# A routed-expert encoder trunk on one core: modulation sums in column quarters, and a router written with comparisons and one scan

## The reference

```python
mod = cond @ w_ada[layer] + b_ada[layer]            # 6 x 1024 values a layer
sh1, sc1, g1, sh2, sc2, g2 = jnp.split(mod, 6, axis=-1)
h = modulate(rms_norm(x, norm1_g[layer]), sh1, sc1)
x = x + g1 * mixer(h)                               # layer 0 attention, layer 1 convolution module
h = modulate(rms_norm(x, norm2_g[layer]), sh2, sc2)
x = x + g2 * moe_ffn(h, ...)
```

## Time and profile before

| | us |
|---|---|
| median of the 3 runs (2121.23 to 2124.85) | 2123.42 |
| the profiled execution, its own time | 2121.78 |
| its span from first to last instruction | 2119.7 |
| PE busy in the span | 1919.2 (91%) |
| DVE busy | 1201.3 (57%) |
| ACT busy | 493.6 (23%) |
| POOL busy | 303.2 (14%) |

### The profile page before, as it was taken

The page is one execution under the profiler, slowest core; times in us unless marked ns, Lnnn a source line. Parts: engine busy times, 40 slices in busy tenths (PEclk is TensorE's granted clock), DMA queues, the critical chain, the costliest instruction groups (busy, mean ns, idle before and its releaser), DMA issues.

```text
span 2119.7 us, 49706 instructions
## 1 busy us (share of the span) xinstructions
PE 1919.2 (91%) x19544; PEld 1163.5 (55%) x19544; DVE 1201.3 (57%) x2175; ACT 493.6 (23%) x1042; POOL 303.2 (14%) x464
## 2 busy tenths in 40 slices
PE   5999999999999946999999579999899399999990
PEld 3444444455666634777777457655445266666660
DVE  3466600378899764333433469999994534333436
ACT  3101100356777630000000230000544000000002
POOL 0001030000000012222222400000001122222223
PEclk9999999799999977999999789999999699999995
DMA  9466520100440087877985803033107599864446
GB/s 397 164 248 256 211 61 0 41 11 11 160 159 11 11 332 264 298 263 260 351 329 216 311 30 105 1 117 107 50 0 267 203 407 407 325 239 170 169 171 253
DMA packets 122490, 391.41 MB, mean 185 GB/s; under 512 B 23808, under 2 KB 44928, under 8 KB 118272
## 3 DMA queue, kind: packets, MB, share of 16 engines
q1 hardware_dynamic: 72432, 303.48, 37.9%
q0 software_dynamic: 21904, 66.99, 8.7%
q10 hardware_dynamic: 28032, 19.17, 3.0%
HBM read 337.33 MB, written 47.49 MB: 182 GB/s over the span
## 4 chain that ended last, share of the span: by engine, by line
PE 84%; DVE 8%; DMA 4%; ACT 1%; issue 1%; SPq 0%; POOL 0%; ACTq 0%; DVEq 0%; POOLq 0%
PE ps L1578 23%; PE ps L1588 12%; PE ps L1420 10%; PE ps L1633 10%; PE ps L1473 5%; PE ps L1529 5%; PE ps L1487 4%; PE ps L1500 4%; PE ps L1512 4%; DVE kv L1302 3%; PE ps L1705 3%; DMA kv<-in_w_ada 1%; PE ps L1670 1%; PE ps L1399 1%; ACT hT L639 1%
## 5 line engine op out<-in xcount | busy, mean ns | idle before, releaser
L1578 PE MATMUL ps<-kv,hT 128*32 128x256 f32 x5504 | 387.2, 380 | 3.4 <-DMA kv<-in_w_gate_up 3.4
L1302 DVE SCALAR_TENSOR_TENSOR kv<-kv,cols 128x640 f32<-128x640 f32 (+1 forms) x330 | 266.2, 807 | 11.2
L1578 PEld LDWEIGHTS ps<-kv,hT 128*32 128x32 f32 x5504 | 229.8, 111 | 77.0 <-issue 5.2
L1176 DVE TENSOR_TENSOR hT<-hT,modc 128x256 f32<-128x256 f32 x146 | 62.1, 425 | 303.8 <-PE ps L1578 303.7
L1633 PE MATMUL ps<-hT,ring 128*128 128x320 f32 (+1 forms) x768 | 225.4, 455 | 6.3 <-ACT hT L639 6.3
L1420 PE MATMUL ps<-hT,ring 128*128 128x512 f32 x512 | 224.5, 597 | 1.6 <-ACT hT L639 1.6
L745 ACT ACTIVATE hT<-ps 128x128 f32<-128x128 f32 x146 | 40.4, 277 | 759.2 <-PE ps L1578 759.2
L1012 DVE TENSOR_TENSOR_SCAN pbuf<-hT 128x128 f32<-128x128 f32 (+7 forms) x128 | 173.2, 1353 | 47.0 <-ACT hT L690 46.7
L1633 PEld LDWEIGHTS ps<-hT,ring 128*128 128x128 f32 x768 | 146.3, 192 | 81.9 <-ACT hT L639 6.9
L1578 PE MATMUL ps<-ring,hT 128*32 128x256 f32 x2560 | 150.6, 387 | 19.7 <-issue 18.0
L1420 PEld LDWEIGHTS ps<-hT,ring 128*128 128x128 f32 x512 | 98.0, 192 | 124.2 <-issue 121.2
(11 more groups left out here) (260 smaller groups left out, 2439.4 us busy)
## 6 DMA issues: line engine op xcount, KB each, us to landing
kv<-in_w_gate_up SPq DMA_DIRECT2D x136, 512.0 KB
kv<-in_w_ada SPq DMA_DIRECT2D x21, 2048.0 KB, 8.1
ring<-in_w_gate_up SPq DMA_DIRECT2D x80, 512.0 KB
kv<-in_w_down SPq DMA_DIRECT2D x48, 512.0 KB
ring<-in_w_down SPq DMA_DIRECT2D x40, 512.0 KB
hT<-in_w_gate_up SPq DMA_DIRECT2D x40, 512.0 KB
expert_rows<-hT ACTq DMA_DIRECT2D x584, 32.0 KB
ring<-in_w_in SPq DMA_DIRECT2D x32, 512.0 KB, 11.3
```

What stands on the lines that cost most here:

```text
L1302: ins = V.scalar_tensor_tensor(new, old, w_dw_c[:, c, k:k + 1], new, ALU.mult, ALU.add)
L1578: ins = mm(bank(0)[UNIT * q:UNIT * (q + 1), 0:2 * P], xT[:, c, :], wset[s][q // 2][:, 512 * c + 256 * (q % 2):512 * c + 256 * (q % 2) + 25 ...
```

## The change

In the modulation, DVE sums four pieces into four buffers (`ada_sum[k]`), and PE takes four at a time: four matmuls with 32-wide weights `ones[:, 0:32]`, each into 32 of the 128 PSUM partitions, after chunks 4, 7, 9, 12 and 14 of Q and K. ACT copies the whole bank, POOL stores four rows. In the router, an expert's rank in its group is the count of the three others that beat it (six comparisons, one reduction), both picked experts come from it at once, the running sum is one scan, and both choices' rows are worked in one instruction. The 0/1 matrices are made 32 wide on the `low` side; PE multiplies them in 128 matmuls with 32-wide weights, a quarter of the table each. PE reads eight of its 16 registers ahead of the table matmuls and eight behind. The matrices move to `hT` below the third weight set; the other scratch stays in `spare`. `square(1, t)` writes to `ring` instead of `bcB` for t below 7, so POOL's reload of `bcB` waits for `x_made`, and SP's load of expert 0's down weights waits for `sq_done`.

```diff
+ADA_GROUPS = REST_ADA // 4
+GROUP_AFTER = (4, 7, 9, 12, 14)
...
-        ada_sum = pbuf[:, :, 0:512]
+        ada_sum = [pbuf[:, k // 2, 512 * (k % 2):512 * (k % 2) + 512] for k in range(4)]
...
-        hots = hflat[:, 4608:8192].bitcast(mybir.dt.bfloat16)
+        hots = hflat[:, 2304:2304 + TT * (3 * UNIT + TABLE)].bitcast(mybir.dt.bfloat16)
...
-            return 0 if cc < 1 else min(REST_ADA, (cc - 1) * REST_ADA // 13)
+            return sum(cc >= after for after in GROUP_AFTER)
...
             sp.wait_ge(av_done, PAIRS)
+            sp.wait_ge(sq_done, 2 * TT - 1)
             first_expert(0, 0, 2)
...
+            def store_rows(g):
+                pool.wait_ge(row_kept, g + 1)
+                for k in range(4):
+                    m = FIRST_ADA + 4 * g + k
+                    pool.dma_start(mod_dram[512 * m:512 * (m + 1)].unsqueeze(0), ada_out[32 * k:32 * k + 1, g % 2, :]
+                                   ).then_inc(row_stored[g % 2], 16)
...
                 if qb:
-                    pool.wait_ge(sq_done, TT + qb)
+                    pool.wait_ge(x_made, 2 * qb)
                 pool.dma_start(bcB[:, :], x[qb * P:(qb + 1) * P, :]).then_inc(x_again, 16)
...
+            def keep_rows(g):
+                if g >= 2:
+                    act.wait_ge(row_stored[g % 2], 64 * (g // 2))
+                act.wait_ge(ada_reduced, g + 1)
+                nc.scalar.activation(ada_out[:, g % 2, :], bank(4 + g % 2), ACT.Copy).then_inc(row_kept, 1)
...
+            def sum_pieces(g, first=False):
+                if not first:
+                    dve.wait_ge(ada_reduced, g)
+                for k in range(4):
+                    u = k % 2
+                    dve.wait_ge(ada_loaded[u], 32 * g + 16 * (k // 2) + 32 - 16 * u)
+                    dve.wait_ge(bias_loaded[u], 32 * g + 16 * (k // 2) + 16)
                     for c in range(DC):
...
+                V.memset(reset[:, :, 1:], 1.0)
+                V.memset(reset[:, :, 0], 0.0)
+                V.memset(route_both[:, :, 0], 0.0)
+                V.memset(zero, 0.0)
+                V.memset(bounds[:, :], 0).then_inc(y_kept[l], 1)
 
                 dve.wait_ge(score_done[l], 1)
...
+                s4 = grouped(sel)
+                for d in range(1, EPG):
+                    V.tensor_tensor(beats[:, :, 0:EPG - d, d - 1], s4[:, :, 0:EPG - d], s4[:, :, d:EPG], ALU.is_lt)
+                    ins = V.tensor_tensor(beats[:, :, d:EPG, EPG - 1 - d], s4[:, :, 0:EPG - d], s4[:, :, d:EPG],
+                                          ALU.is_ge)
                 step(ins)
...
+                step(V.tensor_reduce(grouped(rank), beats, AX.X, ALU.add))
+                step(V.scalar_tensor_tensor(grouped(best), grouped(rank), 2.0, s4, ALU.is_lt, ALU.mult))
+                step(V.tensor_reduce(gs.rearrange("p t g -> p (t g)"), grouped(best), AX.X, ALU.add))
+
+                step(V.tensor_reduce(top, gs, AX.X, ALU.max))
+                step(V.tensor_tensor(same, gs, top.to_broadcast([P, TT, GROUPS]), ALU.is_equal))
+                step(V.tensor_tensor(same, same, pref_g[:, :, :], ALU.mult))
+                step(V.tensor_reduce(top, same, AX.X, ALU.max))
+                step(V.tensor_tensor(group, same, top.to_broadcast([P, TT, GROUPS]), ALU.is_equal))
...
+                both_picked = mark(V.scalar_tensor_tensor(
+                    route_both[:, :, 1:].rearrange("p (g j) t -> p t g j", j=EPG), rank.rearrange(by_group, j=EPG), 2.0,
+                    group.unsqueeze(3).to_broadcast([P, TT, GROUPS, EPG]), ALU.is_lt, ALU.mult))
+                for k in range(2):
+                    V.scalar_tensor_tensor(grouped(chosen[:, k, :, :]), grouped(rank), float(k), in_group, ALU.is_equal,
+                                           ALU.mult)
+                after(both_picked)
...
+                V.tensor_tensor_scan(flat[0], flat[1], flat[2], 0.0, ALU.mult, ALU.add).then_inc(picked[l], 1)
 
                 dve.wait_ge(counted[l], 1)
...
+                picked_rows = mark(V.tensor_tensor(products, first_row.unsqueeze(1).to_broadcast([P, 2, TT, E]), chosen,
+                                                   ALU.mult))
...
+                summed = mark(V.tensor_reduce(wts[:, :, :], products, AX.X, ALU.add))
...
+                V.tensor_scalar(bounds[:, 1:E + 1], ends[0:1, :], 1.0 / UNIT, None, ALU.mult).then_inc(bounds_made[l], 1)
+                after(summed)
+                step(V.tensor_copy(dest[:, :, :], wts[:, :, :]))
...
+                split = mark(V.tensor_tensor(high_hot, lane[:, 0:TABLE].unsqueeze(1).to_broadcast(high),
+                                             slot_i[:, 1, :].unsqueeze(2).to_broadcast(high), ALU.is_equal))
+                after(split)
+                step(V.tensor_tensor(low_hot, lane[:, 0:UNIT].unsqueeze(1).to_broadcast(low),
+                                     slot_i[:, 0, :].unsqueeze(2).to_broadcast(low), ALU.is_equal))
+                V.tensor_scalar(low_row, low_hot, tokid[:, 0:1], None, ALU.mult).then_inc(hot_made[l], 1)
+                by_choice = [ap.rearrange("p (k t) s -> p k t s", k=2) for ap in (low_tile, low_hot)]
+                V.tensor_tensor(by_choice[0], by_choice[1],
+                                tile_first[:, :].unsqueeze(1).unsqueeze(3).to_broadcast([P, 2, TT, UNIT]),
+                                ALU.mult).then_inc(hot_made[l], 1)
                 dve.wait_ge(table_summed[l], 1)
...
-                while reduced < reduced_after(cc) or (cc == 15 and reduced < REST_ADA):
-                    pe.wait_ge(ada_summed, reduced + 1)
+                while reduced < reduced_after(cc):
+                    pe.wait_ge(ada_summed, 4 * reduced + 4)
                     if reduced >= 2:
                         pe.wait_ge(row_kept, reduced - 1)
-                    mm(bank(4 + reduced % 2), ones[:, :], ada_sum[:, reduced % 2, :], start=True,
-                       stop=True).then_inc(ada_reduced, 1)
+                    for k in range(4):
+                        ins = mm(bank(4 + reduced % 2)[32 * k:32 * k + 32, :], ones[:, 0:32], ada_sum[k], start=True,
+                                 stop=True, skip_group_check=True)
+                    ins.then_inc(ada_reduced, 1)
                     reduced += 1
...
                 pe.wait_ge(picked[l], 1)
...
+                mm(bank(5)[:, P:P + E], ones[:, :], route_run[:, :, TT], start=True, stop=True)
+                mm(bank(5)[:, 0:P], upper[:, :], route_both[:, :, 1:].rearrange("p e t -> p t e"), start=True, stop=False)
+                mm(bank(5)[:, 0:P], ones[:, :], route_run[:, :, 0:TT].rearrange("p e t -> p t e"), start=False,
+                   stop=True).then_inc(counted[l], 1)
...
+                pe.wait_ge(bounds_made[l], 1)
+                ends = load_ends(range(E // 2))
+                for k, low in enumerate((low_row, low_tile)):
+                    pe.wait_ge(hot_made[l], k + 1)
+                    for n in range(2 * TT):
+                        for q in range(QUARTERS):
+                            ins = mm(bank(6)[UNIT * q:UNIT * (q + 1), 0:TABLE], low[:, n, :], high_hot[:, n, :],
+                                     start=(n == 0 and k == 0), stop=(n == 2 * TT - 1 and k == 1),
+                                     skip_group_check=True)
                 ins.then_inc(table_summed[l], 1)
+                ends += load_ends(range(E // 2, E))
```

More of the change, by code:

```diff
@@ L1049, in moe, with mark, after, grouped @@
             def moe(l):
[L1050 to L1055 removed]
+                sc, sel, rank, best = (tmp(n) for n in range(4))
+                beats = spare[:, 4 * P:7 * P].rearrange("p (n j s) -> p n j s", j=EPG, s=EPG - 1)
+                chosen = spare[:, 7 * P:9 * P].rearrange("p (k t e) -> p k t e", k=2, t=TT)
+                gs, same, group = (tmp(n, GROUPS) for n in (10, 11, 12))
+                top = tmp(13, 1)
+                padded, ends, zero = (spare[:, (16 + n) * P:(16 + n) * P + E] for n in range(3))
+                first_row = tmp(19)
+                products = spare[:, 20 * P:22 * P].rearrange("p (k t e) -> p k t e", k=2, t=TT)
+                def mark(ins):
+                    steps[0] += 1
+                    ins.then_inc(dve_step, 1)
+                    return steps[0]
+                def after(count):
+                    dve.wait_ge(dve_step, count)
+                def grouped(ap):
+                    return ap.rearrange("p t (g j) -> p (t g) j", j=EPG)
+                V.memset(reset[:, :, 1:], 1.0)
[3 more added lines that the diff above has]
+                V.memset(bounds[:, :], 0).then_inc(y_kept[l], 1)
                 dve.wait_ge(score_done[l], 1)
@@ L1101, in moe @@
-                for t in range(TT):
-                    step(V.tensor_tensor(run[:, t + 1, :], run[:, t, :], both_[:, t, :], ALU.add))
-                V.tensor_copy(b, both_).then_inc(picked[l], 1)
+                after(biased)
+                s4 = grouped(sel)
[3 more added lines that the diff above has]
```

(12 more changed lines are left out.)

187 lines of the change are left out of this document (56 added, 131 removed).

## The result

The kernel after takes 2089.82 us (median of 4 runs, 2087.86 to 2092.98) beside 2122.32 us for the kernel before (4 runs, 2120.57 to 2124.85): a ratio of 0.9847 with a 95% interval of 0.983 to 0.9865, 32.5 us less. The forecast was 2091.7 with a gain of 31.7. The profiled execution took 2088.8 us.

The account below looks back on a forecast made before the run. It took PE's path to bound the kernel: modulation sums, router, layer 1's weight DMA. Gains of 12.6, 11.6 (layer 0) and 7.5 (layer 1) sum to 31.7 us: 2091.7 us, own range 2088 to 2096, 8 in 10 within 2083 to 2102.

Parts of the forecast that it names:

- What bounds the kernel: PE's path: sums between Q and K chunks (17.2 us), the router once a layer, layer 1's weight DMA stretch behind it.
- The modulation sums: Between Q and K chunks: 20 full-width sums become five groups of four quarter matmuls at 0.86 us; gain 12.6 us.
- rival (b): Modulation: a group's sum is late because two loads share the DMA; 6.6 us lost, 2098 us; chance 12%.
- The picks: Router, DVE's choice of experts in each layer: 11.1 us removed, 5.0 added; gain 6.1 us a layer.
- Rival (e): Router: strided and broadcast operands take twice the time per element; 5 us lost a layer, 2102 us; chance 8%.
- From the counts to the table: Router, each layer: 14.0 us becomes 12.65, with 5.4 for the 128 table matmuls; gain 1.4 us.
- rival (a): Table: 32-wide bf16 matmuls take 20 ns, only columns count; 2.6 us instead of 5.4, total 2086 us; chance 25%.
- The register reads: Behind the table: eight remaining reads vanish behind the gather; gain 3.4 us in layer 0, nothing in layer 1.
- End of attention: POOL's earlier reload of bcB spares DVE's wait: gain 0.7 us; SP's new wait costs nothing.
- (c): Modulation: loads land so late that long due times are missed too; slower than before, 2133 us; chance 3%.
- (d): Layer 1: PE's earlier start counts because it pulls the loads with it; 2088 us; chance 7%.

Follow-up runs that it names:

- e3: The kernel after with each group's four quarter matmuls of the modulation issued twice: 2096.83 us, ratio 0.987 to the kernel before.
- e10: The kernel after with three unused rounds of 64 matmul pairs (32-wide bf16 weights; 96, 64, 32 columns) behind the table: 2098.01 us, one run.
- e4: The kernel after with all 16 register reads behind the table matmuls: 2089.45 us, ratio 0.9831 to the kernel before.
- e5: The kernel after with eight register reads behind the table and the other eight each ahead of its expert: 2086.39 us, ratio 0.9821 to the kernel before.
- e6: The kernel after with six more, unused register reads between layer 1's table and its first unit: 2090.62 us, ratio 0.9836 to the kernel before.
- e8: The kernel after with two of expert 2's three weight parts loaded earlier, after the router's scores and last store of h: 2085.53 us, ratio 0.9817.
- e9: The kernel after with the reads of e5 and, in layer 1 alone, the early load of e8: 2078.41 us, ratio 0.9776 to the kernel before.
- e1: The kernel before with the modulation part of the change alone: 2114.13 us, ratio 0.9945 to the kernel before.
- e11: The kernel after with POOL's reload of bcB behind ACT's square again, SP's new wait kept: 2090.09 us, one run.

## Why the prediction was right, and where its terms were off

**What bounds the kernel** held in all three stretches, and the changed kernel gave the time back in each.

**The modulation sums.** Forecast 12.6, measured 11.0, of which 0.2 stand ahead of the first sum. The buffers fitted at three of four due times, and at chunk 9 they were late by the 0.38 us that PE waited. The forecast had a group ready 26.6 us after PE begins to take the one before; there it was ready after some 29.0. It left out that DVE can begin only when the four matmuls are done (1.3 us), and the third piece's load took about 8.8 us and not 8.0. The time between the two groups is longer as well, 28.7 us and not 27.5. So rival (b), a sum that is late, did come, at a small fraction of its price. The larger miss is a group's price, 0.86 us in the forecast and about 1.2 with what the chunks behind it lose. e3 shows that the overlap of the quarters was rightly read from the unit, and that the rest is paid once for each change between full-width weights and quarters. The Trainium skill ("TensorE: Matmul & The Clock Gate", Measured speedup vs the span model) would have priced a group at 1.1 us, nearer to the measured whole; but its reason, 3.07 times for four tiles (measured there with tiles of rows, not of columns), is not what the doubled group shows. Why the chunks behind a group are longer no run settles.

**The picks.** 6.3 us to the scan's end, less 0.2 for the counting matmuls with their strided operand (counts to DVE 1.79 us where it was 1.59): 6.1, as forecast. The scan of 144 elements took 0.45. Rival (e), strides and broadcasts that cost DVE double, falls for the picks as a whole; only the write of both picks in another order (L1115) took 0.39 us, where 128 elements otherwise take 0.29.

**From the counts to the table.** The step that failed in size is the 128 matmuls: 5.4 us were taken, from the row of the float32 logits, and they took 2.75. The rival (a) was right in its mechanism for these 96 columns, the columns alone count, and e10 shows it: 20 ns at 1.2 GHz and 10 to 11 at 2.4; below 64 columns it does not hold. The Trainium skill (same page, LDWEIGHTS) has 27 ns for such a load, 3.4 us for 128; no row here shows it, and with pairs 7.4 to 8.3 ns apart in e10 the loads can't take 27 ns each one after another. The rival's price of 2.8 us a layer was not all collected, because a read takes 0.65 to 0.69 us, not 0.55, and PE began the table 7.75 and 8.04 us behind the counts, 0.8 and 1.1 later than the forecast's 6.95. Measured gain 3.2 and 3.5, forecast 1.4. With the reads moved (e4, e5) PE waits for `low_row`, and counts to table is 8.65 us, less than the 9.85 that the rival would have given.

**The register reads.** In layer 0 the table to the first unit went from 9.17 to 5.58 us, 3.6 for a forecast of 3.4; in layer 1 the start gained 3.3 and the wait for expert 4 grew by 3.6 (3.4 to 7.0). e6 shows from the other side that PE's start does not set that stretch, e8 and e9 that the start of expert 2's load does.

**End of attention.** The 0.7 us at DVE's wait is seen between the two traces, and in e1, which has the reload as before, the wait is there too (0.71 us, landing 8.1). But of it only 0.2 arrives at the router (0.4 between e1 and the kernel after), and with the reload as late as before and SP's new wait kept (e11) nothing is lost. So the forecast's term was too large. Whether SP's later weight loads let the reload land sooner was not tried.

**Between the layers** 1.0 us was lost that the forecast does not have. The first block of the output projection took 15.43 us for its 32 records, 13.74 before, at a mean granted clock of 0.89 where it was 1.00:

```profile
1536.27:1551.70 15.43, 15.43 (x35) 0.89 0.00 1
```

Over all runs the stretch between the layers lies between 829.5 and 832.0 us with no order by the edits. I count it as an execution's own variation.

The sum: -1.6, -0.6, +2.0, -1.0, +2.1 and +0.1 make the 1.0 us by which the profiled gain exceeds the forecast. Of the rivals, (a), given 25%, had the right mechanism for the table; (b) came at one due time, for 0.38 us; (c), (d) and (e) did not come. The forecast's total is closer than its terms are.

## What to carry to other kernels

Read who waits behind a step before pricing it: the same 3.6 us of PE time were worth all in layer 0 and nothing in layer 1, and there it was the start of a load, held by a scratch buffer, that was worth 4.5 us by itself (e8) and 7.0 in e9, 1.7 of these by the clock. An engine's reads of registers from memory are instructions of their own; put them where matmuls are still queued ahead of them or a gather is awaited. When a transfer is started earlier, look for what stands behind it in the queue: here it ran dry until the next buffer was free, and in the other layer it delayed a gather.

## What the runs showed of the hardware

Quarters of 32 columns cost as one in steady state (0.86 us for eight records on 512 columns), but a switch from full-width weights and back costs 0.3 to 0.4 us, once. Small bf16 pairs with 32-wide weights, in four quarters, run at 20 ns on 96 columns and 13 on 64 at 1.2 GHz, at 10 to 11 and 7.4 at 2.4; on 32 columns they gain nothing more and stay at 8.3 ns. Why PE stops now and then within hundreds of such pairs (0.66, 1.77 and in e3 1.13 us) no run tells.

Two waits of nearly the same length left the clock differently. Windows of e8 and of e9, PE's wait for expert 4 and the unit behind it:

```profile
1684.98:1687.18 2.20, 0.00 (x1) 0.03 (x2) 1.39 (x4) 0.00 (x0) 0.33 (x1) 1.00 1.05 416
1687.18:1692.31 5.13, 5.13 (x64) 3.37 (x68) 0.00 (x0) 0.00 (x0) 0.98 (x1) 0.67 1.03 409
```

```profile
1682.21:1684.27 2.06, 0.01 (x2) 0.03 (x1) 1.39 (x4) 0.00 (x0) 0.33 (x1) 1.00 1.05 415
1684.27:1687.72 3.45, 3.45 (x65) 2.51 (x68) 0.00 (x0) 0.00 (x0) 0.98 (x1) 1.00 1.03 405
```

Behind 2.20 us the granted clock fell to a mean of 0.67 over the unit, which took 5.13 us; behind 2.06 us it stayed at 1.00, and the unit took 3.45. That is 1.7 of the 2.5 us by which e9's stretch is shorter than e8's. It is not the length of the wait alone, for in e4 a wait of 2.07 us was followed by a unit that took 5.14 us (the next row's start is 1700.44):

```profile
1695.30 5.35 PE L1606 MATMUL ps<-kv,hT 128*32 128x256 f32 x64 [2.07 <-DMA kv<-in_w_gate_up]
```
